# A hybrid decoder step: key scores end eight blocks early, and value pages begin beside the last v blocks

## The reference

```python
h = rms_norm(x, norm_a) @ w_in_a; b, c, hx, z = split(h, 4)          # first layer
x = x + (b * conv3(c * hx) * silu(z)) @ w_out_a
k, v = split(rms_norm(x, norm_kv) @ w_kv); k = rope(rms_norm(k))       # shared keys and values
q, z = split(rms_norm(x, norm_b) @ w_in_b); q = rope(rms_norm(q))      # second layer
p = softmax(q @ [k_past, k]^T, masked)                                 # two maps a head
o = (p[0] - lam * p[1]) @ [v_past, v]                                  # pages picked by page_table
x = x + ((rms_norm(o) * (1 - lam_init)) * silu(z)) @ w_out_b
```

## Time and profile before

| | us |
|---|---|
| median of 3 runs | 2569.31 (2566.92 to 2569.72) |
| the profiled execution | 2572.17 |
| its span, first to last instruction | 2570.4 |
| TensorE busy, of the span | 2473.9 (96%) |
| VectorE busy | 1505.0 (59%) |
| ScalarE busy | 1016.5 (40%) |
| GpSimd busy | 345.6 (13%) |

### The profile page before, as it was taken

One profiled execution on the slowest core, in us unless ns is written; L12 is line 12 of the kernel. 1 busy time (PEld: TensorE's weight loads), 2 busy tenths in 40 slices (PEclk: granted clock), 3 DMA queues, 4 the chain that ended last, 5 costly groups with the idle time before them and its releaser, 6 DMA issues.

```text
span 2570.4 us, 51030 instructions
## 1 busy us (share of the span) xinstructions
PE 2473.9 (96%) x20963; PEld 2165.8 (84%) x20963; DVE 1505.0 (59%) x1663; ACT 1016.5 (40%) x1832; POOL 345.6 (13%) x137
## 2 busy tenths in 40 slices
PE   8999999999999999999999999999999788789999
PEld 7999999999999999899999999998999433245565
DVE  5665566666564333455788878776767465543211
ACT  4111111121111223767545477875555344331111
POOL 4323233323230111000000000000000022220000
PEclk9999999999999999999999999999999888899999
DMA  5223233223222333234577887878888899989995
GB/s 155 83 82 97 82 83 97 82 82 98 82 82 87 120 108 101 79 119 152 161 261 261 274 275 245 278 256 284 295 298 278 310 365 377 394 311 376 381 336 216
DMA packets 376326, 520.52 MB, mean 203 GB/s; under 512 B 16553, under 2 KB 311858, under 8 KB 357682
## 3 DMA queue, kind: packets, MB, share of 16 engines
q1 hardware_dynamic: 314434, 461.55, 52.6%
q10 hardware_dynamic: 61600, 56.45, 6.5%
q0 software_dynamic: 128, 0.26, 0.0%
HBM read 483.46 MB, written 34.75 MB: 202 GB/s over the span
## 4 chain that ended last, share of the span: by engine, by line
PE 83%; DMA 5%; ACT 5%; DVE 4%; issue 2%; SPq 1%; ACTq 0%; POOL 0%; DVEq 0%; POOLq 0%
PE psum L112 25%; PE psum L1292 16%; PE psum L120 12%; PE psum L1300 8%; PE psum L1889 7%; PE psum L1343 4%; PE psum L1963 3%; DMA heads<-out_new_v_prompt_dram 2%; ACT w_raw L1057 1%; PE psum L1942 1%; DMA w_raw<-in_w_in_b_dram 1%; PE psum L1924 1%; DVE h_keys_turned L1235 1%; PE psum L1308 1%; DMA w_raw<-in_w_kv_dram 1%
## 5 line engine op out<-in xcount | busy, mean ns | idle before, releaser
L1292 PE MATMUL psum<-x_hi,w_hi 128*128 128x272 f32 x2048 | 433.6, 293 | 0.0
L112 PE MATMUL psum<-x_hi,w_hi 128*128 128x272 f32 x2048 | 427.2, 289 | 2.2 <-DVEq L446 2.2
L112 PE MATMUL psum<-x_lo,w_hi 128*128 128x272 f32 x2048 | 426.2, 290 | 0.0
L1292 PE MATMUL psum<-x_lo,w_hi 128*128 128x272 f32 x2048 | 425.2, 289 | 0.0
L1292 PEld LDWEIGHTS psum<-x_hi,w_hi 128*128 128x128 f32 x2048 | 321.3, 189 | 16.6 <-issue 16.3
L112 PEld LDWEIGHTS psum<-x_hi,w_hi 128*128 128x128 f32 x2048 | 321.6, 190 | 2.7 <-issue 2.3
L1292 PEld LDWEIGHTS psum<-x_lo,w_hi 128*128 128x128 f32 x2048 | 321.5, 188 | 0.0
L112 PEld LDWEIGHTS psum<-x_lo,w_hi 128*128 128x128 f32 x2048 | 321.0, 188 | 0.0
L1235 DVE STREAM_TRANSPOSE h_keys_turned<-h_ring 128x1024 f32<-128x1024 f32 x256 | 299.7, 1214 | 19.9 <-DMA h_ring<-in_cache_k_dram 11.4
L399 POOL TENSOR_TENSOR w_raw<-w_raw,params 128x2048 f32<-128x2048 f32 x63 | 238.9, 3793 | 507.3 <-DMA w_raw<-in_w_in_a_dram 507.3
L1300 PE MATMUL psum<-x_hi,w_lo 128*128 128x272 f32 x2048 | 285.7, 295 | 0.0
(11 more groups left out here) (214 smaller groups left out, 3015.4 us busy)
## 6 DMA issues: line engine op xcount, KB each, us to landing
h_ring<-in_cache_k_dram SPq DMA_DIRECT2D x256, 512.0 KB, 6.7
ring<-in_cache_v_dram SPq DMA_DIRECT2D x128, 1024.0 KB, 7.9
w_raw<-in_w_in_a_dram SPq DMA_DIRECT2D x64, 1024.0 KB, 6.2
w_raw<-in_w_kv_dram SPq DMA_DIRECT2D x16, 2048.0 KB, 13.4
w_raw<-in_w_in_b_dram SPq DMA_DIRECT2D x15, 2048.0 KB, 9.6
w_raw<-in_w_out_a_dram SPq DMA_DIRECT2D x16, 1024.0 KB, 5.6
wo_raw<-in_w_out_b_dram SPq DMA_DIRECT2D x8, 2048.0 KB, 11.4
ring<-in_w_out_b_dram SPq DMA_DIRECT2D x16, 1024.0 KB, 6.8
```

The lines of the kernel that those rows point to most:

```text
L112: pe.matmul(out[:, g, 0:GT], m.WH[s][:, k * P:(k + 1) * P], x[:, k * T + g * GT:k * T + (g + 1) * GT], start=(k == 0 and x is xh), stop=Fa ...
L1292: pe.matmul(psum[n % 2][:, g, 0:GT], m.WH[n % 2][:, k * P:(k + 1) * P], x[:, k * T + g * GT:k * T + (g + 1) * GT], start=(k == 0 and x is ...
```

## The change

- `UNITS_IN_STEP` is now 3, 4, 3, 4, ... in the z blocks from 18 on, 3 in each k block, 4 in v blocks 48 to 54 and 3 in block 55. Blocks 56 to 63 use 22 value pages instead (`PAGES_IN_STEP`), from a ring that lies in the freed key ring and stays there; 106 pages are left behind.
- Two softmaxes (sequences 0 and 1) are spread over blocks 50 to 62, each within six blocks. The output of sequence 0 is turned in block 62 and taken out by VectorE there; its new tokens' part is a product of its own, `first_new`, after page 27, which VectorE adds (`add_first_new`).
- The z gate is finished on ScalarE: Ln(1 + e) and Exp(-...), in `norm_scale`, in place of VectorE's add and reciprocal.
- The scratch store leaves `store(n-3)` and becomes `keep(n-2)`, after laying and moving and ahead of the scaling.
- A head has seven pages for its nine sub-steps: `parts_at` puts 0 and 1 behind its first page and 4 and 5 behind its fourth. The tail has 5, 5 and ten times 4 pages. `hops` gives the places of the softmax pieces.
- `load_inner` is split. `load_queries(r)` is issued near the end of head r-2, `load_values(r)` at the start of head r-1; the scores wait for the first only and `prompt_out` for the second. Those of head 1 are issued when block 63 is done, ahead of the last v block's store.

```diff
-UNITS_IN_STEP = [2, 3] * 8 + [3, 3, 3, 2] * 4 + [3, 3, 4, 3, 4, 3, 3, 4, 3, 4, 3, 4, 3, 0]
-SOFT_STEP = 3 * KT + 4
-OUT = 6
-assert sum(UNITS_IN_STEP) == UNITS
+UNITS_IN_STEP = [3, 4] * 7 + [3] * KT + [4] * 7 + [3]
+SOFT_STEPS = [3 * KT + 2, 3 * KT + 8]
+FIRST_PAGE_STEP = FIRST_UNIT_STEP + len(UNITS_IN_STEP)
+PAGES_IN_STEP = [3, 3, 3, 2, 3, 2, 3, 3]
+EARLY_PAGES = sum(PAGES_IN_STEP)
+NR = 5
+OUT, TRN = 6, 7
+assert sum(UNITS_IN_STEP) == UNITS and FIRST_PAGE_STEP + len(PAGES_IN_STEP) == len(KINDS) * KT
+assert FIRST_PAGE_STEP == SOFT_STEPS[0] + 6 and sum(PAGES_IN_STEP[:6]) == NPG
...
+def pages_of(n):
+
+    at = n - FIRST_PAGE_STEP
+    if not 0 <= at < len(PAGES_IN_STEP):
+        return {}
+    first, many = sum(PAGES_IN_STEP[:at]), PAGES_IN_STEP[at]
+    return dict(zip({2: "AC", 3: "ABC"}[many], range(first, first + many)))
...
-        return len(KINDS) * KT
+        return FIRST_PAGE_STEP + 1
...
+    def load_page(self, sp, n, src, dst):
+        after(sp, self.v_used, n - NR + 1)
+        sp.sem_inc(self.m.granted, 1)
+        sp.dma_start(dst, src).then_inc(self.page_in[n % NR], 16)
+
+    def use_page(self, pe, v, ring):
+
+        i, p = v // NPG, v % NPG
+        if p == 0:
+            pe.wait_ge(self.wt_ready, i + 1)
+            after(pe, self.osb_ready, i)
+        pe.wait_ge(self.page_in[v % NR], 16 * (v // NR + 1))
+        for c in range(4):
+            last = pe.matmul(self.m.PS[c * TURN:c * TURN + 2 * NEW, OUT, :], self.wt[i % 2][:, weights_at(p, c):weights_at(p, c) + 2 * NEW],
+                             ring[v % NR][:, c * 512:(c + 1) * 512], start=(p == 0), stop=(v == NPG - 1), skip_group_check=True)
+        last.then_inc(self.v_used, 1)
...
+    def take_rows(self, act, i):
+
+        if i == 0:
+            act.wait_ge(self.v_used, NPG)
+        else:
+            act.wait_ge(self.out_done, i)
+        after(act, self.o_turned, i + (i >= 2))
+        act.activation(self.osb[:, :], self.m.PS[:, OUT, :], ACT.Copy).then_inc(self.osb_ready, 1)
...
+    def turn_rows(self, pe, i):
+
+        pe.wait_ge(self.osb_ready, i + 1)
+        after(pe, self.out_taken, i + (i >= 1))
...
+    def first_new(self, pe):
+
+        pe.wait_ge(self.out_taken, 1)
+        pe.wait_ge(self.wtn_ready, 1)
+        for t in range(4):
+            last = pe.matmul(self.m.PS[:, TRN, t * TURN:(t + 1) * TURN], self.vnew[:, t * P:(t + 1) * P], self.wtn4[0],
+                             start=True, stop=True, skip_group_check=True)
+        last.then_inc(self.o_turned, 1)
+
+    def add_first_new(self, dve):
+
+        dve.wait_ge(self.o_turned, 2)
+        for t in range(4):
+            kept = self.ost[:, :].rearrange("p (c t x) -> p c t x", c=4, t=4)[:, :, t, 0:NEW]
+            new = self.m.PS[:, TRN, t * TURN:(t + 1) * TURN].rearrange("p (c x) -> p c x", c=4)[:, :, (t // 2) * NEW:(t // 2 + 1) * NEW]
+            ins = dve.tensor_tensor(kept, new, kept, ALU.add)
+        ins.then_inc(self.out_taken, 1)
...
+            def load_values(v):
+
+                page = sp.value_load(pages[0:1, v:v + 1], min_val=0, max_val=n_phys - 1)
+                if v < 4:
+                    sp.wait_ge(kt_ready, 2 * UNITS - 5 + v // 2 * 4 + v % 2)
+                elif v < NR:
+                    sp.wait_ge(unit_scored, UNITS - 1)
+                soft.load_page(sp, v, cache_v[ds(page, 1), :, :].rearrange("o p n -> (o p) n"), values[v % NR])
...
+                if n == FIRST_PAGE_STEP - 1:
+                    for v in range(NR):
+                        load_values(v)
+                for v in pages_of(n).values():
+                    load_values(v + NR)
...
-            def store(n):
+            def keep(n):
                 s, kind, local = n % 2, kind_of(n), n % KT
                 if kind != "v":
                     act.wait_ge(tile_ready, kept_before(n) + 1)
                     act.dma_start(scratch[kind][local].rearrange("p (g t) -> p g t", g=G),
                                   grouped(tile[s][:, :])[:, :, 0:GP]).then_inc(scratch_out[s], 16)
+
+            def store(n):
+                kind, local = kind_of(n), n % KT
...
-                    act.activation(r[s][:, :], plain[s][:, :], ACT.Exp, scale=-1.0).then_inc(r_step, 2)
+                    act.activation(r[s][:, :], plain[s][:, :], ACT.Exp, scale=-1.0).then_inc(r_step, 1)
 
             def norm_scale(n):
                 if normed(n):
                     act.wait_ge(summed, norms_before(n) + 1)
-                    rsqrt(act, r_step, n * 2, psum[n % 2][:, :, 0:GT], HD, m, grouped(r[n % 2][:, :]))
+                    rsqrt(act, r_step, r_before(n), psum[n % 2][:, :, 0:GT], HD, m, grouped(r[n % 2][:, :]))
+                elif kind_of(n) == "z":
+                    act.wait_ge(r_step, r_before(n) + 1)
+                    act.activation(r[n % 2][:, :], r[n % 2][:, :], ACT.Ln, bias=m.ONES[:, 0:1], scale=1.0).then_inc(r_step, 1)
+                    act.wait_ge(r_step, r_before(n) + 2)
+                    act.activation(r[n % 2][:, :], r[n % 2][:, :], ACT.Exp, scale=-1.0).then_inc(r_step, 1)
...
+                if NPG in pages_of(n).values():
+                    soft.take_rows(act, 0)
                 if n + 1 < N:
                     split_hi(n + 1)
                 if n == 0:
                     one.norm()
+                for i, at in enumerate(SOFT_STEPS):
+                    if n == at + 4:
+                        soft.exp(act, i)
+                    if n == at + 6:
+                        soft.group_new(act, i)
+                        soft.load(act, i + 1, half_out)
                 if n >= 3:
                     store(n - 3)
                 if n >= 1:
@@ -1163,16 +1292,13 @@
                     lay_queries(lays[n])
                 if n in moves:
                     move_scores(moves[n])
-                if n == SOFT_STEP:
-                    act.wait_ge(tile_ready, 3 * KT)
+                if n >= 2:
+                    keep(n - 2)
+                if n == SOFT_STEPS[0] - 1:
                     soft.load(act, 0, half_out)
-                if n == SOFT_STEP + 7:
-                    soft.exp(act, 0)
                 if n % 2 == 0 and n + 2 < N:
                     scale_pair(n // 2 + 1)
-            soft.group_new(act, 0)
-            soft.load(act, 1, half_out)
-            two.store, two.move_scores = store, move_scores
...
-                    chain.link(dve.tensor_scalar(r[s][:, :], r[s][:, :], 1.0, None, ALU.add))
-                    chain.link(dve.reciprocal(r[s][:, :], r[s][:, :]))
...
+                for i, at in enumerate(SOFT_STEPS):
+                    if n == at + 1:
+                        soft.max(dve, i)
+                    if n == at + 2:
+                        soft.diag(dve, i)
+                    if n == at + 3:
+                        soft.shift(dve, i)
+                    if n == at + 4:
+                        soft.sum(dve, i)
+                    if n == at + 5:
+                        soft.weights(dve, i)
                 for at in "BCD":
                     if at in units:
                         turn_unit(units[at])
-            turn_scores(UNITS // 4 - 1)
-            dve.memset(m.PS[:, OUT, :], 0.0).then_inc(out_blank, 1)
+                if n == FIRST_PAGE_STEP - 1:
+                    dve.memset(m.PS[:, OUT, :], 0.0).then_inc(out_blank, 1)
+                if n == FIRST_PAGE_STEP:
+                    turn_scores(UNITS // 4 - 1)
+                if NPG + 2 in pages_of(n).values():
+                    soft.take_out(dve, 0)
...
+            def use_values(v):
+                soft.use_page(pe, v, values)
+                if v == NPG + 1:
+                    pe.wait_ge(sct_ready, UNITS // 4)
+                    soft.turn_rows(pe, 0)
...
+                if "A" in using:
+                    if n == FIRST_PAGE_STEP:
+                        pe.wait_ge(out_blank, 1)
+                    use_values(using["A"])
...
-    HP = 9
-    BPS = [5] * 8 + [4] * 4
...
+    V0 = EARLY_PAGES
+    HP, SUBS = 7, 9
+    BPS = [5] * 2 + [4] * 10
...
+        def parts_at(j):
+
+            return [k for k in range(SUBS) if k * HP // SUBS == j]
+
+        def hops(i):
+
+            if i == 1:
+                return dict(max=6, turn=9, diag=9, spread=10, shift=10, exp=11, sum=12, sums=13, weights=14, group=15)
+            return dict(max=2, turn=4, diag=5, spread=6, shift=7, exp=8, sum=9, sums=11, weights=13, group=14)
...
-                after(act, o_done, r - 1)
+                after(act, prompt_scored, (r - 1) * TT)
                 if r == 0:
                     act.wait_ge(two.block_done, two.N - 2)
                     for f in range(2):
                         act.wait_ge(two.scratch_out[f], 16 * two.kept[f])
-                act.wait_ge(two.rows_out, 32 * (two.turns - KT + min(2 * r + 2, KT - 2)))
-                if r == H - 1:
-                    act.wait_ge(two.last_out, 64)
                 if r == 1:
                     act.wait_ge(two.block_done, two.N)
```

(32 more changed lines are left out.)

230 lines of the change are left out of this document (108 added, 122 removed).

## The result

The changed kernel takes 2615.08 us (median of 4 runs, 2614.43 to 2617.17) against 2569.51 for the kernel before beside it: ratio 1.0161, 95% interval 1.0145 to 1.0178. It is slower by 45.6 us, where I had forecast 2582, slower by 13. The profiled execution took 2617.17 us, its span is 2615.4.

The account below looks back on a forecast made before the run. TensorE was taken to bound the kernel except among the heads, paced by VectorE and ScalarE chains. Second stage +40.4, heads -21.4, tail -6.0 sum to +13.0 us: 2585.2 profiled, 2582.3 median; range 2572 to 2596, widened to 2555 to 2597.

Parts of the forecast that it names:

- Second stage, the work: Weight blocks: 22 value pages, small matmuls and score units add 27.4 us; old stalls go; net +12.4 us.
- Second stage, the waits: New TensorE stalls in z, k and v, mostly from late ScalarE work: 28 us, bounds 4 and 38.
- The limit of +23.6: Even z blocks: upper part needed by 23.6 us after block start; forecast 25.8 in blocks 26, 28 and 30.
- Each stall over 2 us lowers the clock: +2.: Second stage: slower TensorE clock after each stall over 2 us, priced at 2 us in all.
- The first head: Loads ready -11.0 us, two pages fewer -2.0, new wait +9.5 (bounds 0 and 17).
- The wait that I had named: First head: TensorE waits for the new sample values, 9.5 us, bounds 0 and 17.
- The other heads: Seven heads: two pages fewer each give 2.2 us a head, 15.4 in all; less softmax work gives 2.5.
- The tail: Six pages fewer and half a chain less, with page 80 waiting 5 us instead of 2.7: -6, bounds -11 and -3.
- The reciprocal: z blocks: ScalarE gains 3.9 us for Ln, Exp and two table loads; VectorE loses 3.55 us, no trouble.
- The waits don't come: Rival: ScalarE finishes double blocks 2 to 3 us sooner, new waits about 4 us; total -11, 2558 us; chance 0.27.
- What would show it: Stalls at blocks 27, 29, 31, 39, 47, 49, new-values wait in first head, heads of 27.5 to 30 us, page 80 wait.
- sign of being wrong: Either second stage growing by under 20 us, or heads below 27 us.

Follow-up runs that it names:

- the run of three cures: Changed kernel with queries laid a block earlier in six blocks, second-unit keys transposed ahead of v's softmax step, and eight pages a head: 2582.62 us, ratio 1.0036.

## Why the prediction was right or wrong

The sign was right, the size was not: +45.6 against +13, and the time lies outside the range. Two terms make up most of the difference of 32 us: what pages give back when they leave the heads (14.7 us too much), and the low clock behind the stalls of the second stage (some 10 too little). By the steps of the sum:

- *Second stage, the work: +27.4 for pages, small groups and units, less 15 of old stalls.* In the blocks without a stall a unit costs 1.1 to 1.2 us, as forecast. The whole is right within some 3 us, as far as the next two items let it be read.
- *Second stage, the waits: 28, bounds 4 and 38.* The stage grew by 55.7 us, not 40.4. TensorE's idle time in blocks 18 to 63 rose from 10.6 to 30.7 us. I had 26 us of waits without the clock: 4.7 too few. The limit of +23.6 was right: the upper parts of 26, 28 and 30 came at +25.1, +26.5 and +25.1 (forecast 25.8), and blocks 27, 29 and 31 waited 1.5, 2.8 and 1.4 us, which is by how much these missed the limit. In k the size was luck in part: blocks 39 and 47 waited 3.4 each (forecast 2.9), and ScalarE was late there for the reason forecast, since laying a block earlier removed the wait. But 3.25 of the 3.4 are TensorE's wait for the square, which my sum did not have, and not the wait for keys that it had. Block 49 took 28.0 us, 10.6 more than a block of four units without a stall, 6.9 of it idle (forecast 10). Not foreseen were block 23, whose pair came at +18.4, and blocks 50 to 53, where VectorE's softmax step stood ahead of the keys. I had read VectorE's busy sum there and not its order. Block 23's 3.6 us stand in z's total where I had 2 us for four other pairs, so that total (9.3 us idle, forecast 9) is luck too. Why this pair was late stays open: the 16 engines were as full in block 24 (1.04), whose pair had landed by +12.4.
- *"Each stall over 2 us lowers the clock: +2."* This is the term that failed in the stage. If the 27.4 of work is right, 55.7 - 27.4 - 20.1 = 8.2 us are net of the 4.4 of before, so 12.6 us lie behind stalls at the low clock. Block by block it comes to about the same: what blocks 23, 29, 39, 47, 49 and 51 took beyond a like block's 16.8 us in z, 17.2 in k and 17.4 in v, and beyond their own idle time, is 1.7 to 3.7 us each and some 14 in all (a few small softmax matmuls in it), while blocks 27 and 31, which stood for 1.5 and 1.4 us, have 0.1 each. The same reading gives 3.1 for the kernel before, and leaves some 24 for the work. The earlier trace rows had the price (2.2 us idle, then 1.5 more in the next block), and I counted it about once for six blocks with such stalls.
- *The first head: -11.0 - 2.0 + 9.5.* -3.5 forecast, -2.6 measured. In the changed kernel the 9 us were a blocked issue on ScalarE. The wait that I had named was hidden behind it, and came out at 6.1 and 12.5 us in two runs whose profiled executions were slow ones, and at 4.3 in the run of three cures. The size was right for the wrong row, which is luck; that something in the first head makes up for the split loads' gain is real.
- *The other heads: -15.4 for two pages fewer each, -2.5 for a chain less.* This is the step that failed most: -17.9 forecast, -3.2 measured. I had argued page by page from what stood behind it, and wrote that in busier heads all of a page is won. But TensorE already stood 33.1 us in these heads for mixed weights, in 14 places, and when 15.3 us of work had left, it stood 15.0 us longer. In a stretch paced by another chain, work taken off TensorE turns into waiting. My first paragraph says that these chains set the pace among the heads; the price of a page forgot it. The rows of that wait were there to be read before the forecast.
- *The tail: -6.* -5.6 measured, with page 80's wait 4.83 us (forecast 5).
- *The reciprocal.* VectorE was no trouble with it on ScalarE, and would have been with it at home (3.5 us). Ln and Exp with a table load each were worth their price. Both loads stand in the changed kernel's z blocks (timeline of block 29), so the trace disagrees with the Trainium skill (ScalarE: Activation LUTs, section "Table sets: the hidden batching unit") here as well:

```profile
1444.29 1.28 ACT L1231 ACT_TABLE_LOAD   x1
1445.58 0.75 ACT L1231 ACTIVATE work<-work,ones 128x544 f32<-128x544 f32 x1
1446.35 1.28 ACT L1233 ACT_TABLE_LOAD   x1
...
1447.65 0.66 ACT L1233 ACTIVATE work<-work 128x544 f32<-128x544 f32 x1
```

- *The rivals.* "The waits don't come" is out: upper parts at +25.1 and later. What I lacked was a rival in which the heads give nothing: +40.4 - 3.5 - 6.0 = +31, and with the clock at its real price over +40. The measured time fits that sum, which is made after the fact.
- *What would show it.* The stalls at 27, 29, 31, 39, 47, 49 and page 80 were there, those at 39 and 47 ended by the square and not by key transposes. The wait for the new values was not, in the changed kernel, and the heads of 27.5 to 30 us came out at 28.7 to 33.8. Neither sign of being wrong came (a stage that grows by under 20 us, heads below 27): both watched only the fast side.

## What to carry to other kernels

Before moving work off a stretch, read in the waits view what the engine stands for there. If it is another engine's chain, the moved work was almost free where it was, and is paid in full where it goes: here the 22 pages cost some 26 us (an estimate, at the 1.17 us of the forecast) in a full stage, 14 of them came out of seven heads that got 3.2 us shorter together, and only the six from the tail paid. Price each stall of 2 to 4 us with the slow time that follows it (here 1.7 to 3.7 us), and where transfers are sent ahead, follow each issue in that engine's program order.

## What the runs showed of the hardware

- Issuing a transfer can hold up the engine: 2.64, 6.03 and 1.49 us for three issues in a row on ScalarE with head 1's loads ahead in the queue, 0.39, 1.30 and 1.14 us with its 0.5 MB of values behind them. That the queue was full is my reading; no row shows its length. SyncE had the same in the kernel before (timeline): four issues of keys ahead of that of a 2 MB weight pair took 3.71 us, the two behind it 6.63.

```profile
1398.98 3.71 SPq L1010 DMA_DIRECT2D h_ring<-in_cache_k_dram  x4
1402.82 0.39 SPq L998 DMA_DIRECT2D w_raw<-in_w_in_b_dram  x1
1404.12 6.63 SPq L1010 DMA_DIRECT2D h_ring<-in_cache_k_dram  x2
```

- When TensorE had stood still for 3.3 to 3.6 us, its mean granted clock was 0.66 to 0.73 over the 10 to 12 us that began with the stall, which cost about 2.5 us more. Blocks that stood for 1.4 and 1.5 us took 0.1 us beyond that. Taking 33 us of filler work from the heads took the clock there from 0.85 to 0.72.
- Four matmuls of a value page, on four partition groups, take 1.04 us together (0.97 to the next work in the chain of waits); one of them alone took 1.03, so leaving three out did not free TensorE.
